# Turning the FFN's input with VectorE and small SBUF transfers instead of TensorE, and another order of work at the entry of the pool mixer

## The chip, the cores and the metric

The kernel runs on one core of a Trainium2 chip, in one launch. The metric is the device time of that core in microseconds. The core has five engines that run their own instruction queues in order: TensorE (PE, with its weight loads as PEld), VectorE (DVE), ScalarE (ACT), GpSimd (POOL) and SyncE (SP, which here issues nearly all DMA transfers). They wait for each other through semaphores.

## The reference

Two blocks follow each other on x of 1024 rows and 1024 columns, all in fp32. The first block is latent attention beside an mLSTM, then an FFN, then a gated per-layer embedding. The second block is a pooling mixer with a layer norm. What bears on the change:

```python
mix = jnp.concatenate([mla_out, mlstm_out], axis=-1) @ w_out[i]
h = h + rms_norm(mix, attn_post_norm[i])

f = rms_norm(h, ffn_pre_norm[i])
f = (jax.nn.silu(f @ w_gate[i]) * (f @ w_up[i])) @ w_down[i]
h = h + rms_norm(f, ffn_post_norm[i])
h = h + jax.nn.sigmoid(h @ w_ple_gate[i]) * (p[i] @ w_ple_proj[i])
# second block
h = x @ w_in                      # pool_mixer: 1024 x 4096
u, z = h[..., :D_POOL], h[..., D_POOL:]
outs.append((c - lag) / cnt - u[:, :, g])   # windowed means of u
```

## The kernel before

Matrix products are made with each fp32 operand split in a rounded part (hi, fp32r) and a rest (lo), as three products hi*hi, hi*lo, lo*hi (`three`). The big products of FFN and pool mixer use a seven-product scheme for 2x2 blocks (`quad`): a quad has seven block products o = 0 to 6 of 12 matmuls each. Products 4, 5 and 6 are added onto the banks in which products 0, 2 and 3 lie, so before each of them ACT must have copied that bank out (`copy_product`, counted by `prod_copied`), and DVE adds the copies up (`quad_sums`, counted by `quad_summed`).

**Output projection and FFN input.** The loop over the eight row tiles t of 128 rows works so. PE makes `mixed(t, 0)` and `mixed(t, 1)`, 24 matmuls each, into two PSUM banks that alternate between even and odd t. ACT takes the squares of the result with the 1024 x 128 tile `h1_blk` as a throwaway output (L2397), DVE scales it into `h1_blk` (L3191) and adds `x_blk` (L3195, `h1_ready`), splits the mixer rows of tile t+2 (`split_mix`), ACT takes squares again (L2403), and DVE writes `f_blk` = the FFN's input rows (L3201, `rows_ready`). PE then transposes `f_blk` by eight 128x128 products with the identity (`f_transposed`, L1731) into PSUM. ACT copies the result twice (`take_f`: L2385 to `f_full`, L2387 to the rounded part), and DVE subtracts to get the rest (`split_f`, L3182). PE transposes tile t-1 after `mixed(t, 1)`, and tile 7 inside the second gate block.

`x_blk` and `h1_blk` are single buffers. SP's program for tile t waits for `h1_ready`, spills `h1_blk` to DRAM (L889, `h1_spilled`), and loads `x_blk` for tile t+1 (L891, `xblk_in`). ACT's L2397 of tile t+1 waits for the spill of tile t (`act.wait_ge(h1_spilled, 16 * t)`), and DVE's L3195 waits for `x_blk`. PE's `mixed(t)` waits for L3191 of tile t-2 (`mix_taken`) and for the split of tile t (which stands behind L3195 of tile t-2).

**Pool entry.** The first two quads of the pool mixer (`N_QUADS`, `N_QUADS + 1`) start while the last gate product of the first block is still being used. The sums of x blocks that they need (`x_sums`, L3446 to L3452), their rounded parts (`x_sum_hi`, L2553) and rests (`x_sum_lo`, L3489) are made just in time. PE's order there is o = 0, 4, sum product 2, o = 5, sum product 1, and then the second quad with sum products 3 and 6 in between. ACT's order is written out by hand: rounded parts of x sums, copies of products (L2573), rounded parts of weights (`pool_block_hi`, `next_hi`, L2548), `silu` (L2639). POOL makes the rest of each weight block (L1327) after ACT has made its rounded part. DVE runs the x sums, the weight sums, `quad_sums` (L3256, L3260, L3262, L3275) and `window_rows` (L3538 to L3544) in one fixed order.

Of the kernel before, what the change touches and what calls it, by code (L numbers as in the profile page):

```python
# [25 lines left out]
P = 128  # L26
S = 1024
D = 1024
# [61 lines left out]
def build(nc, a, out):  # L90
    ctx = ExitStack()
    with ctx:
# [32 lines left out]
        def col(n):  # L125
# [117 lines left out]
            for j, name in enumerate(("e_buf", "d_t", "inter", "s_t", "q_in", "k_w")))  # L243
# [15 lines left out]
                 (r_10, r_01), f_part[0][1]]  # L259
        f_raw = [f_00, f_11, f_01, at("fs_raw3", [P, 4, HALF], Z)]  # L260
# [253 lines left out]
        def pool_landed(q):  # L514

            return 32 * ((12, 10)[q % 2] + q // 2 + 1)

# [163 lines left out]
        def sp_program(sp):  # L681
# [297 lines left out]
            def x3_store(i, n):  # L979

                sp.wait_ge(xr_ready, 4 * i + 2 * n + 2)
# [50 lines left out]
            for n in range(2):  # L1032
                sp.wait_ge(xr_stored[n], 64 * 4)
# [344 lines left out]
        def pe_program(pe):  # L1378
# [346 lines left out]
            def f_transposed(t):  # L1725
                pe.wait_ge(rows_ready, 8 + t + 1)
                if t >= 2:
                    pe.wait_ge(rows_split, 16 + 2 * t - 2)
                for k in range(KD):
                    b = 4 + 2 * (t % 2) + k // 4  # L1730
                    last = tr(ps[:, b, (k % 4) * P:(k % 4 + 1) * P], f_blk[:, k * P:(k + 1) * P], ident[:])  # L1731
                    if k % 4 == 3:
                        last.then_inc(rows_full, 1)
# [173 lines left out]
            def sum_product(o, at):  # L1907
# [6 lines left out]
                (w_h, w_l), (x_h, x_l) = ring[o], x_sum[i]  # L1914
                dst = ps[:, bank_of[o], :]
                for k in range(4):
                    cs = slice(k * P, (k + 1) * P)
                    mm(dst, w_h[:, cs], x_h[:, k, :], start=(o < 4 and k == 0), stop=False, skip_group_check=(o >= 4))
                    mm(dst, w_l[:, cs], x_h[:, k, :], start=False, stop=False, skip_group_check=(o >= 4))
                pe.wait_ge(xs_split, i + 1)  # L1920
                for k in range(4):
                    last = mm(dst, w_h[:, k * P:(k + 1) * P], x_l[:, k, :], start=False, stop=(k == 3),
                              skip_group_check=(o >= 4))
                last.then_inc(prod_full, 1)

# [9 lines left out]
            quad(N_QUADS, 0, x_factors, (0, 4), x_sums)  # L1935
            sum_product(2, 2)
# [82 lines left out]
        def act_program(act):  # L2019
# [371 lines left out]
            for t in range(TB):  # L2391
# [200 lines left out]
            def first_block_rows(i):  # L2592
                q = N_QUADS + 2 * i
                if i == 0:
                    act.wait_ge(xr_stored[1], 64 * 4)
                else:
                    act.wait_ge(m_stored[0], 16 * i)
# [11 lines left out]
            for i in range(8):  # L2609
# [17 lines left out]
                act.wait_ge(quad_summed, IN_SUMS + 4 * q + 2)  # L2627
                copy_product(q + 1, 4, 0)
                next_hi(q + 1, 0, 1)
                copy_product(q + 1, 4, 1)  # L2630
                next_hi(q + 1, 2)
                copy_product(q + 1, 4, 2)
                next_hi(q + 1, 3)
# [81 lines left out]
        def dve_program(dve):  # L2715
# [461 lines left out]
            def split_f(t):  # L3177
                for j in range(2):
# [3 lines left out]
                    v.tensor_tensor(f_l[:, :, ts], ps[:, 4 + 2 * (t % 2) + j, :].rearrange("p (k n) -> p k n", k=4),  # L3182
                                    f_h[:, :, ts].bitcast(F32), ALU.subtract).then_inc(rows_split, 1)
# [3 lines left out]
            for t in range(TB):  # L3187
# [15 lines left out]
                if t >= 1:  # L3203
                    split_f(t - 1)
# [250 lines left out]
            def x3_turned(j):  # L3455
# [3 lines left out]
                if i:  # L3459
                    dve.wait_ge(xr_stored[n], 64 * i)  # L3460
# [59 lines left out]
            dve.wait_ge(xr_stored[0], 64 * 4)  # L3520
# [8 lines left out]
            dve.wait_ge(xr_ready, 16)  # L3529
            dve.wait_ge(xr_stored[1], 64 * 4)  # L3530
# [293 lines left out]
```

## Time and profile before

| | |
|---|---|
| median of 3 runs | 1797.97 us (1797.95 to 1798.09) |
| the profiled execution's own time | 1797.84 us |
| its span, first to last instruction | 1796.0 us |
| granted TensorE clock, mean | 0.999 |
| busy: PE, DVE, POOL, ACT | 1777.2, 1410.6, 1102.2, 690.0 us |
| DMA | 206.53 MB, mean 115 GB/s |

The span is 1.8 us shorter than the execution's own time. PE is busy for 99% of the span, so the views that matter are those that tell in which stretches PE works on something that could go elsewhere, where it stands still, and what the other engines would do if it did not. Times of rows are in us from the start of the span; a row of the timeline gives the start, the duration, engine, line, operation, output<-input, shape and count, and in brackets the idle time of that engine before it and what ended it.

### The profile page before, as it was taken

The page shows a single profiled execution, that of the slowest core. Times are in us where ns is not written, and L with a number is a line of the kernel's source. Part 1 is how long each engine was busy: PE and PEld are TensorE (multiplying, and loading weights), DVE is VectorE, ACT ScalarE, POOL GpSimd, SP SyncE. Part 2 cuts the span into 40 slices and gives each one's busy share as a digit, 9 for nine tenths or more (in the row PEclk, how much of TensorE's full clock was granted, in tenths as well). Part 3 has the DMA queues.
Part 4 walks back from the last instruction along what each step waited for, and adds up shares of the span by engine and source line. Part 5 has one row for each costly group of instructions (what it writes and reads, how often), then busy time and mean ns, then how long its engine had stood idle before and what let it go on. Part 6 is the DMA issues. An engine that isn't in the chain of part 4 may idle for free.

```text
span 1796.0 us, 22436 instructions
## 1 busy us (share of the span) xinstructions
PE 1777.2 (99%) x8398; PEld 1485.6 (83%) x8398; DVE 1410.6 (79%) x1665; ACT 690.0 (38%) x1211; POOL 1102.2 (61%) x772
## 2 busy tenths in 40 slices
PE   9999999999999999999999999999999999999998
PEld 8888888888888888888888888887788888888886
DVE  7889877766696658666599989679888875798896
ACT  6555577843431111111233334414433343333314
POOL 4066632360399979888778778633655465567554
PEclk9999999999999999999999999999999999999999
DMA  7342410032303323233375631133232231943232
GB/s 210 95 154 57 126 34 17 22 125 94 128 27 103 129 71 118 96 116 117 106 281 179 231 129 48 48 98 90 94 123 100 106 141 71 366 173 107 73 102 94
DMA packets 142718, 206.53 MB, mean 115 GB/s; under 512 B 48897, under 2 KB 104833, under 8 KB 138897
## 3 DMA queue, kind: packets, MB, share of 16 engines
q1 hardware_dynamic: 142434, 205.03, 34.0%
q8 instruction: 67, 1.10, 0.2%
q14 instruction: 41, 0.34, 0.1%
q10 hardware_dynamic: 176, 0.07, 0.0%
HBM read 151.51 MB, written 53.04 MB: 114 GB/s over the span
## 4 chain that ended last, share of the span: by engine, by line
PE 77%; DVE 1%; ACT 1%; issue 0%; POOL 0%; DVEq 0%; ACTq 0%
PE ps L1392 68%; PE ps L1744 2%; PE ps L1746 2%; PE ps L1745 2%; PE ps L1978 1%; PE ps L1977 1%; PE ps L1979 1%; PE ps L1865 0%; ACT xs_hi L2553 0%; PE ps L1645 0%; PE ps L1731 0%; PE ps L1620 0%; PE ps L1635 0%; DVE xs_lo L3489 0%; POOL ring_lo L1327 0%
## 5 line engine op out<-in xcount | busy, mean ns | idle before, releaser
L1392 PE MATMUL ps<-f_hi,ring_hi 128*128 128x512 f32 x368 | 143.5, 390 | 0.0
L1392 PE MATMUL ps<-f_lo,ring_hi 128*128 128x512 f32 x368 | 143.3, 389 | 0.0
L1392 PE MATMUL ps<-f_hi,ring_lo 128*128 128x512 f32 x368 | 143.3, 389 | 0.0
L1238 POOL TENSOR_TENSOR ring_lo<-w_sum,ring_hi 128x512 fp32r<-128x512 f32 x84 | 128.4, 1529 | 7.0
L1392 PE MATMUL ps<-d_w_hi,d_hid_hi 128*128 128x512 f32 x312 | 121.6, 390 | 0.0
L2427 ACT ACTIVATE f_copy<-ps 128x512 f32<-128x512 f32 x63 | 37.3, 596 | 219.4 <-PE ps L1392 211.6
L1392 PE MATMUL ps<-d_w_hi,d_hid_lo 128*128 128x512 f32 x312 | 121.5, 389 | 0.0
L1392 PE MATMUL ps<-d_w_lo,d_hid_hi 128*128 128x512 f32 x312 | 121.5, 389 | 0.0
L1392 PE MATMUL ps<-f_low,ring_hi 128*128 128x512 f32 x336 | 117.2, 389 | 0.0
L1327 POOL TENSOR_TENSOR ring_lo<-w_sum,ring_hi 128x512 fp32r<-128x512 f32 x56 | 87.6, 1574 | 40.7 <-ACT ring_hi L2548 40.6
L1237 POOL TENSOR_SCALAR ring_hi<-w_sum 128x512 fp32r<-128x512 f32 x84 | 79.1, 942 | 31.3 <-PE ps L1392 30.2
L1392 PE MATMUL ps<-xs_lo,ring_hi 128*128 128x512 f32 x240 | 93.4, 389 | 0.0
L1392 PE MATMUL ps<-xs_hi,ring_hi 128*128 128x512 f32 x240 | 93.4, 389 | 0.0
L1392 PE MATMUL ps<-xs_hi,ring_lo 128*128 128x512 f32 x240 | 93.4, 389 | 0.0
L1237 POOL TENSOR_SCALAR ring_hi<-stage 128x512 fp32r<-128x512 f32 x37 | 34.2, 924 | 90.3 <-PE ps L1746 84.4
L1327 POOL TENSOR_TENSOR ring_lo<-stage,ring_hi 128x512 fp32r<-128x512 f32 x24 | 35.4, 1479 | 78.2 <-ACT ring_hi L2548 78.1
L1392 PEld LDWEIGHTS ps<-f_hi,ring_hi 128*128 128x128 f32 x368 | 69.1, 188 | 14.3
L1392 PEld LDWEIGHTS ps<-f_lo,ring_hi 128*128 128x128 f32 x368 | 69.1, 188 | 14.3
L1392 PEld LDWEIGHTS ps<-f_hi,ring_lo 128*128 128x128 f32 x368 | 69.1, 188 | 14.3
L1392 PE MATMUL ps<-x_hi,ring_hi 128*128 128x512 f32 x192 | 75.3, 392 | 4.7 <-ACT x_copy L2573 4.3
L1118 POOL TENSOR_TENSOR w_lo<-stage,w_hi 128x1024 fp32r<-128x1024 f32 x30 | 75.2, 2506 | 2.5
L2460 ACT ACTIVATE d_hid_hi<-d_raw 128x1024 fp32r<-128x1024 f32 x37 | 39.1, 1060 | 96.0 <-PE ps L1392 96.0
(574 smaller groups left out, 5859.8 us busy)
## 6 DMA issues: line engine op xcount, KB each, us to landing
d_raw<-hid_rows SPq DMA_DIRECT2D x37, 512.0 KB, 4.4
stage<-in_w_up SPq DMA_DIRECT2D x22, 512.0 KB, 4.6
wd_raw<-in_w_down SPq DMA_DIRECT2D x22, 512.0 KB, 5.0
raw_w<-in_w_gate SPq DMA_DIRECT2D x20, 512.0 KB, 4.9
stage<-in_pool_w_in SPq DMA_DIRECT2D x16, 512.0 KB, 4.9
raw_w<-in_pool_w_in SPq DMA_DIRECT2D x16, 512.0 KB, 4.7
m_rows<-u_row SPq DMA_DIRECT2D x16, 512.0 KB, 2.6
z_rows<-z_buf SPq DMA_DIRECT2D x8, 1024.0 KB, 4.1
```

Of the source, the lines that this page charges most:

```text
L1118: g.tensor_tensor(lo, stage[:, h, :], hi.bitcast(F32), ALU.subtract).then_inc(parted[h], 1)
L1237: pool_hi.do(pool, g.tensor_scalar(view(hi), src, 1.0, 0.0, ALU.mult, ALU.add))
L1238: g.tensor_tensor(view(lo), src, view(hi).bitcast(F32), ALU.subtract).then_inc(w_split, 1)
L1327: g.tensor_tensor(as_blocks(lo, src), src, as_blocks(hi, src).bitcast(F32), ALU.subtract).then_inc(w_split, 1)
L1392: last = mm(out_ap, l, r, start=(start and j == 0), stop=(stop and j == n - 1), skip_group_check=onto)
L1744: mm(o, l_hi, w_hi[s][:, c:c + HALF], start=(k == 0), stop=False)
L1745: mm(o, l_hi, w_lo[s][:, c:c + HALF], start=False, stop=False)
L1746: last = mm(o, l_lo, w_hi[s][:, c:c + HALF], start=False, stop=(k == 7))
L1977: mm(ps[:, m, :], w_hi[1][:, c:c + P], x_h, start=(k == 0), stop=False)
L1978: mm(ps[:, m, :], w_hi[1][:, c:c + P], x_l, start=False, stop=False)
L2427: f(copies[:, j, :], ps[:, bank0 + bank_of[o], :], ACT.Copy).then_inc(prod_copied, 1)
L2460: f(d_hid[s % 4][0][:], d_raw[s % 6][:], ACT.Copy).then_inc(d_hi, 1)
```

## The change

For rows tiles 0 to 5 (`TURNED = 6`) PE no longer transposes `f_blk`. DVE transposes it in 32x32 blocks into one of two new buffers (`f_turned`, 128 x 1024), and SP moves the blocks to their places in `f_full` with 16 transfers of 32 KB from SBUF to SBUF, each with runs of 128 bytes. ACT then makes the rounded part from `f_full` instead of from PSUM (one copy for each half instead of two), and DVE the rest. `take_f` and `split_f` work two tiles behind instead of one. Tiles 6 and 7 are transposed by PE as before. At the pool entry PE makes the rounded part of sum product 2 ahead of o = 4 and its rest behind it, and ACT's copies stand in another order: before the second to fourth rounded parts of x sum 1, and in the second quad after the first instead of the second sum of the quad before.

```diff
@@ sp_program, in the loop over t, behind the load of x_blk
+                if t < TURNED:
+                    sp.wait_ge(xr_ready, t + 1)
+                    for c in range(4):
+                        for b in range(4):
+                            rows = f_full[32 * c:32 * c + 32, :, t * P + 32 * b:t * P + 32 * b + 32]
+                            turned = f_turned[t % 2][32 * b:32 * b + 32, :].rearrange("c (k a r) -> c k a r", k=KD, r=32)
+                            sp.dma_start(rows, turned[:, :, c, :], **SMALL).then_inc(xr_stored[t % 2], 16)
@@ pe_program
             for t in range(2, TB):
                 pe.wait_ge(mix_taken, t - 1)
                 mixed(t, 0)
-                if t == 2:
-                    f_transposed(0)
                 mixed(t, 1)
-                f_transposed(t - 1)
+                if t > TURNED:
+                    f_transposed(t - 1)
...
-            quad(N_QUADS, 0, x_factors, (0, 4), x_sums)
-            sum_product(2, 2)
+            quad(N_QUADS, 0, x_factors, (0,), x_sums)
+            sum_high(2, 2)
+            quad(N_QUADS, 0, x_factors, (4,), x_sums, at=1)
+            sum_low(2)
@@ act_program
             def take_f(t):
                 for j in range(2):
+                    if t < TURNED:
+                        act.wait_ge(xr_stored[t % 2], moved(t))
+                        f(f_part[j][t // 4][0][:, :, (t % 4) * P:(t % 4 + 1) * P],
+                          f_full[:, 4 * j:4 * j + 4, t * P:(t + 1) * P], ACT.Copy).then_inc(rows_hi, 2)
+                        continue
...
-                if t >= 1:
+                if 1 <= t <= TURNED:
+                    act.wait_ge(xr_ready, t)
+                elif t:
                     act.wait_ge(rows_full, 16 + 2 * t)
...
-                if t >= 1:
-                    take_f(t - 1)
+                if t >= 2:
+                    take_f(t - 2)
+            take_f(TB - 2)
             take_f(TB - 1)
...
-            x_sum_hi(0, (0, 1, 2))
+            x_sum_hi(0)
             act.wait_ge(w_split, IN_BLOCKS + blocks_split(N_QUADS) + 7)
             copy_product(N_QUADS, 0, 0)
-            x_sum_hi(0, (3,))
             x3_part(15)
-            x_sum_hi(1)
+            x_sum_hi(1, (0,))
             copy_product(N_QUADS, 0, 1)
+            x_sum_hi(1, (1, 2, 3))
...
-                act.wait_ge(quad_summed, IN_SUMS + 4 * q + 2)
+                act.wait_ge(quad_summed, IN_SUMS + 4 * q + (2 if i else 1))
                 copy_product(q + 1, 4, 0)
+                if i == 0:
+                    next_hi(q + 1, 0)
+                    act.wait_ge(quad_summed, IN_SUMS + 4 * q + 2)
+                    copy_product(q + 1, 4, 1)
+                    copy_product(q + 1, 4, 2)
+                    next_hi(q + 1, 1, 2, 3)
@@ dve_program, in the loop over t, behind L3201
-                if t >= 1:
-                    split_f(t - 1)
+                if t < TURNED:
+                    dve.wait_ge(rows_ready, 8 + t + 1)
+                    if t >= 2:
+                        dve.wait_ge(xr_stored[t % 2], moved(t - 2))
+                    v.transpose(f_turned[t % 2][:], f_blk[:]).then_inc(xr_ready, 1)
+                if t >= 2:
+                    split_f(t - 2)
+            split_f(TB - 2)
             split_f(TB - 1)
```

## Rows read from the trace of the kernel before

**Rows 1.** The page's first part: busy us, share of the span, instructions.
```profile
PE 1777.2 (99%) x8398; PEld 1485.6 (83%) x8398; DVE 1410.6 (79%) x1665; ACT 690.0 (38%) x1211; POOL 1102.2 (61%) x772
```
**Rows 2.** Timeline around one transposition by PE (tile 1).
```profile
421.98 0.40 PE L1746 MATMUL ps<-w_hi,mix_lo 128*128 128x512 f32 x1
...
422.21 1.04 PE L1731 MATMUL ps<-ident,f_blk 128*128 128x128 f32 x8
...
423.00 0.47 PE L1744 MATMUL ps<-w_hi,mix_hi 128*128 128x512 f32 x1
```
**Rows 3.** Timeline of SP for one tile, and landing of a spill.
```profile
438.36 0.33 SPq L889 DMA_DIRECT2D h_rows<-h_blk  x1
438.73 0.43 SPq L891 DMA_DIRECT2D x_blk<-in_x_lanes  x1
...
h_rows<-h_blk SPq DMA_DIRECT2D x8, 512.0 KB, 2.9
```
**Rows 4.** SP's timeline where it issued 16 transfers from SBUF to SBUF.
```profile
45.94 5.04 SPq L743 DMA_DIRECT2D rot<-cos_q  x8
51.02 3.33 SPq L743 DMA_DIRECT2D rot<-neg_sin_q  x4
54.40 2.49 SPq L743 DMA_DIRECT2D rot<-sin_q  x4
56.93 1.13 SPq L687 DMA_DIRECT2D stage<-in_w_in  x2
```
**Rows 5.** Issues of other small transfers by tile: ns min/median/max.
```profile
L784 SPq DMA_DIRECT2D wqr_h<-in_w_uq x6: 434/469/470, 235.4 to 237.9; - x6
L986 SPq DMA_DIRECT2D x_rows<-x_turned x32: 303/498/1034, 1167.0 to 1252.9; - x32
```
**Rows 6.** Tile 0 of `f_blk` (timeline), and DVE's block transposes (by tile).
```profile
411.34 1.29 DVE L3201 SCALAR_TENSOR_TENSOR f_blk<-h_blk,cols,ffn_gain 128x1024 f32<-128x1024 f32 x1
...
L3462 DVE STREAM_TRANSPOSE x_turned<-pp x16: 698/703/706, 1160.8 to 1250.8; 128x512 f32<-128x512 f32 x16
```
**Rows 7.** Timeline of tiles 6 and 7, from the product to the transposition.
```profile
469.57 1.02 ACT L2397 ACTIVATE h_blk<-ps 128x1024 f32<-128x1024 f32 x1 [4.29 <-PE ps L1746]
...
481.37 1.03 ACT L2397 ACTIVATE h_blk<-ps 128x1024 f32<-128x1024 f32 x1 [4.31 <-PE ps L1746]
...
487.14 1.29 DVE L3201 SCALAR_TENSOR_TENSOR f_blk<-h_blk,cols,ffn_gain 128x1024 f32<-128x1024 f32 x1
...
488.35 1.28 DVE L3182 TENSOR_TENSOR f_lo<-ps,f_hi 128x512 fp32r<-128x512 f32 x2
488.48 0.86 PEld L1731 LDWEIGHTS ps<-ident,f_blk 128*128 128x128 f32 x8 [0.56 <-DVE f_blk L3201]
```
**Rows 8.** PE's timeline at the pool entry, the rows with idle time before them.
```profile
1237.23 0.47 PE L1392 MATMUL ps<-x_hi,ring_hi 128*128 128x512 f32 x1 [0.84 <-ACT x_copy L2573]
...
1244.33 0.47 PE L1392 MATMUL ps<-x_hi,ring_hi 128*128 128x512 f32 x1 [1.38 <-ACT x_copy L2573]
...
1267.56 0.47 PE L1392 MATMUL ps<-x_hi,ring_hi 128*128 128x512 f32 x1 [1.20 <-ACT x_copy L2573]
1271.46 0.47 PE L1392 MATMUL ps<-x_hi,ring_hi 128*128 128x512 f32 x1 [0.93 <-ACT x_copy L2573]
```
**Rows 9.** Timeline of DVE, ACT, POOL and PE up to the third quad.
```profile
1252.89 2.29 DVE L3489 TENSOR_TENSOR xs_lo<-xs_raw,xs_hi 128x2048 fp32r<-128x2048 f32 x1 [1.44 <-ACT xs_hi L2553]
...
1284.42 0.63 ACT L2639 ACTIVATE z_buf<-z_buf 128x512 f32<-128x512 f32 x1 [10.28 <-DVE z_buf L3262]
...
1286.62 1.45 POOL L1327 TENSOR_TENSOR ring_lo<-stage,ring_hi 128x512 fp32r<-128x512 f32 x1 [10.60 <-ACT ring_hi L2548]
...
1288.13 0.50 PE L1392 MATMUL ps<-x_hi,ring_hi 128*128 128x512 f32 x1
```
**Rows 10.** DVE's timeline: four x sums, without and with a POOL operation beside them.
```profile
1248.35 2.48 DVE L3450 TENSOR_TENSOR xs_raw<-pp 128x512 f32<-128x512 f32 x4
...
1255.10 3.59 DVE L3452 TENSOR_TENSOR xs_raw<-pp,xs_raw 128x512 f32<-128x512 f32 x4
```

More of the change, by code:

```diff
@@ L259, in build @@
                  (r_10, r_01), f_part[0][1]]
+        f_turned = [at(f"f_turned{i}", [P, D], Z + 4 * KB * i) for i in range(2)]
         f_raw = [f_00, f_11, f_01, at("fs_raw3", [P, 4, HALF], Z)]
@@ L516, in pool_landed, with moved @@
             return 32 * ((12, 10)[q % 2] + q // 2 + 1)
+        TURNED = 6
+        MOVED = TURNED // 2 * 16 * 16
+        def moved(t):
+            return 16 * 16 * (t // 2 + 1)
         X3_SPLIT = [j for j in range(16) if not (j < 8 and j % 4 >= 2)]
@@ L979, in x3_store @@
             def x3_store(i, n):
-                sp.wait_ge(xr_ready, 4 * i + 2 * n + 2)
+                sp.wait_ge(xr_ready, TURNED + 4 * i + 2 * n + 2)
                 for b in range(4):
@@ L1032, in sp_program @@
             for n in range(2):
-                sp.wait_ge(xr_stored[n], 64 * 4)
+                sp.wait_ge(xr_stored[n], MOVED + 64 * 4)
             for b in range(4):
@@ L1732, in f_transposed @@
                     if k % 4 == 3:
-                        last.then_inc(rows_full, 1)
+                        last.then_inc(rows_full, 2 * TURNED + 1 if t == TURNED and k == 3 else 1)
             def mixed(t, e):
@@ L1905, in pe_program, with sum_high @@
             sum_of = {2: 0, 1: 1, 3: 2, 6: 3}
-            def sum_product(o, at):
+            def sum_high(o, at):
                 i = sum_of[o]
@@ L1913, in sum_product @@
                 pe.wait_ge(xs_hi_ready, 4 * i + 4)
-                (w_h, w_l), (x_h, x_l) = ring[o], x_sum[i]
+                (w_h, w_l), x_h = ring[o], x_sum[i][0]
                 dst = ps[:, bank_of[o], :]
@@ L1919, in sum_product, with sum_low @@
                     mm(dst, w_l[:, cs], x_h[:, k, :], start=False, stop=False, skip_group_check=(o >= 4))
+            def sum_low(o):
+                i = sum_of[o]
                 pe.wait_ge(xs_split, i + 1)
                 for k in range(4):
-                    last = mm(dst, w_h[:, k * P:(k + 1) * P], x_l[:, k, :], start=False, stop=(k == 3),
-                              skip_group_check=(o >= 4))
+                    last = mm(ps[:, bank_of[o], :], ring[o][0][:, k * P:(k + 1) * P], x_sum[i][1][:, k, :], start=False,
+                              stop=(k == 3), skip_group_check=(o >= 4))
                 last.then_inc(prod_full, 1)
+            def sum_product(o, at):
+                sum_high(o, at)
+                sum_low(o)
             def x_sums(o):
@@ L2594, in first_block_rows @@
                 if i == 0:
-                    act.wait_ge(xr_stored[1], 64 * 4)
+                    act.wait_ge(xr_stored[1], MOVED + 64 * 4)
                 else:
@@ L2626, in act_program @@
                     next_hi(q, 4, 5, 6)
-                act.wait_ge(quad_summed, IN_SUMS + 4 * q + 2)
+                act.wait_ge(quad_summed, IN_SUMS + 4 * q + (2 if i else 1))
                 copy_product(q + 1, 4, 0)
[L2629 to L2633, printed above, removed]
+                if i == 0:
[4 more added lines that the diff above has]
+                    next_hi(q + 1, 1, 2, 3)
+                else:
+                    next_hi(q + 1, 0, 1)
+                    copy_product(q + 1, 4, 1)
+                    next_hi(q + 1, 2)
+                    copy_product(q + 1, 4, 2)
+                    next_hi(q + 1, 3)
                 if i == 7:
@@ L3181, in split_f @@
                     f_h, f_l = f_part[j][t // 4]
-                    v.tensor_tensor(f_l[:, :, ts], ps[:, 4 + 2 * (t % 2) + j, :].rearrange("p (k n) -> p k n", k=4),
-                                    f_h[:, :, ts].bitcast(F32), ALU.subtract).then_inc(rows_split, 1)
+                    src = ps[:, 4 + 2 * (t % 2) + j, :].rearrange("p (k n) -> p k n", k=4)
+                    if t < TURNED:
+                        src = f_full[:, 4 * j:4 * j + 4, t * P:(t + 1) * P]
+                    v.tensor_tensor(f_l[:, :, ts], src, f_h[:, :, ts].bitcast(F32), ALU.subtract).then_inc(rows_split, 1)
             split_mix(0, 1)
@@ L3202, in dve_program @@
                                        ALU.mult, ALU.mult).then_inc(rows_ready, 1)
[L3203 to L3204 removed]
+                if t < TURNED:
+                    dve.wait_ge(rows_ready, 8 + t + 1)
[5 more added lines that the diff above has]
+            split_f(TB - 2)
             split_f(TB - 1)
@@ L3459, in x3_turned @@
                 if i:
-                    dve.wait_ge(xr_stored[n], 64 * i)
+                    dve.wait_ge(xr_stored[n], MOVED + 64 * i)
                 turned = x_turned[n][:].rearrange("p (t m c) -> p m t c", m=2, c=32)[:, j % 2]
@@ L3519, in dve_program @@
                 x_sums(3, k)
-            dve.wait_ge(xr_stored[0], 64 * 4)
+            dve.wait_ge(xr_stored[0], MOVED + 64 * 4)
             second_sums((2,))
@@ L3527, in pool_sums @@
                 block_sums(N_QUADS + q, w_sum[q % 2], 3 - q % 2)
-            dve.wait_ge(xr_ready, 16)
-            dve.wait_ge(xr_stored[1], 64 * 4)
+            dve.wait_ge(xr_ready, TURNED + 16)
+            dve.wait_ge(xr_stored[1], MOVED + 64 * 4)
             for c in range(2):
```

## The prediction, made before the changed kernel was run

> **What bounds the kernel now.** I read the page's busy shares first, then PE's waits, then the timeline of two stretches. PE is busy for 99% of the span [rows 1]; the reader is to see that only two things shorten this kernel, matmuls that leave PE and stalls of PE. The longest stalls by cause are four waits for ACT's copies of products at the pool entry, 4.35 us in all [rows 8]. In the output projection PE never waits, and it spends part of its time on transposing. So both parts of the change aim at PE. The question is what the other queues do with their new work.
>
> **What goes from PE.** Between the last matmul of one half of the mixer and the first after the transposition lie 1.02 us; one matmul step is 0.23, so eight transposes hold 0.79, and the matmul behind them takes 0.47 in place of 0.39 [rows 2]. That is 0.87 us for one tile, and six tiles leave PE: 5.2 us.
>
> **What comes to SP.** For each of six tiles SP issues, behind the spill and the load of `x_blk`, 16 transfers, and the next tile's spill stands behind them in its queue. Spill and load themselves take 0.37 + 0.47 = 0.84 us of SP [rows 3]. A transfer from SBUF to SBUF of this size has rows in this trace: 16 of 32 KB over 32 partitions each, issued back to back, from 45.94 to the next issue at 56.93 [rows 4]. So 16 cost 10.99 us of SP: 0.63 each for the eight and the last four, and one group of four that took 0.84 longer. Other small transfers were cheaper to issue: 256 runs of 128 bytes from DRAM took a median of 0.47 (0.51 with the gap), 512 runs of 256 bytes to DRAM 0.50 [rows 5], thus 8.2 to 8.6 us for 16. I take 10.99, because it is the only row with SBUF at both ends, and the new transfers have the same bytes and partitions; their 256 runs instead of 32 could make it more. The bounds are 8.2 and, at 1.03 each as the slowest of [rows 5], 16.5 us.
>
> **What SP's time does to the end of the stage.** I follow SP's queue. Tile 0 of `f_blk` is written at 412.6 and its block transpose takes twice 0.70, so the first transfers start at 414.0 [rows 6]. A turn of SP is then 10.99 + 0.84 = 11.8 us. PE's turn is 11.80 (from L2397 of tile 6 to that of tile 7 [rows 7]), less 0.87 without transposes = 10.9 us. SP is the slower one and has no gap: h1 and the block transpose of each tile are ready before SP comes to them (tightest is tile 2: the spill of tile 1 starts at 425.0 and lands at 427.9; from L2397 to `f_blk` it is 7.1 [rows 7], under 1 for the split of mixer rows, 1.4 for the block transpose, so 437.3, and SP gets there at 437.7). Six sets of transfers and five pairs of spill and load end at 414.0 + 66.0 + 4.2 = 484.2. There the spill of tile 6 starts, lands 2.9 later [rows 3] at 487.1, and only then may ACT overwrite `h1_blk` for tile 7, which it did at 481.37 before [rows 7]. The last tile's chain is therefore 5.7 us later than before, although PE came to its end 5.2 us earlier. Everything that was taken from PE is spent in waits within `mixed` and behind the first gate block.
>
> **One more wait at the end.** PE's transposition of tile 7 waits until the rests of tile 5 are made. Before, DVE had made them a tile earlier. Now `split_f(5)` stands in tile 7's turn behind `f_blk`, 1.28 us [rows 7]. In PE's queue behind it stands the rest of the gate block, and for that all of the FFN. The stall of 0.56 there becomes 1.28 longer. The sum for the stage is +5.7 + 1.3 = +7.0 us. ACT's work falls (two copies for a tile instead of four) and DVE gets 1.4 more for a tile; both have 4.3 us of idle time in a turn, as ACT's 4.31 shows [rows 7], so they cost nothing. If that cover were gone each would cost 1.4 a tile. The landing of a tile's transfers isn't awaited for two turns, 22 us, and a spill of as many bytes lands in 2.9 [rows 3].
>
> **If the transfers are cheaper.** The same sum gives the point of decision: the stage costs nothing when 6B + 414.0 + 4.2 + 2.9 = 481.37 - 1.28, that is at B = 9.8 us for 16. Up to about 8.5 us nothing waits and the stage gives -5.2 + 1.3 = -3.9. At 16.5 it would be +7.0 + 6 x 5.5 = +40.
>
> **Pool entry.** The four waits are 0.84, 1.38, 1.20 and 0.93 [rows 8]. The first goes, since 8 matmuls now stand before the product that waits. Of the second about 0.9 stays: the copy can start only when the rest of sum product 2 is through. The third and fourth go, since their copies no longer stand behind DVE's second sum. PE would be 3.5 us ahead. But it can't keep that. Product 4 of the third quad started at 1288.13 right on POOL's rest of its weights, which waited 10.60 for ACT's rounded part, which stood behind the `silu` that waited 10.28 for DVE's sum [rows 9]. Nothing of this order is changed, and DVE works without a gap from 1252.89 to that sum. So what counts is how much earlier DVE starts at 1252.89, where it waited 1.44. The rounded parts that it waits for now come with DVE's own sums, which end some 0.7 later than before because `x_sum_lo(1)` has to wait for the parts that were moved behind the copy. That leaves -0.7. Against it, POOL's second block of that quad moves from DVE's idle time onto the four x sums, and such a meeting costs 3.59 - 2.48 = 1.1 [rows 10]. I take -0.3; the bounds are -2.0, all that DVE idles in this stretch with the 1.44, and +2.2, two such meetings more.
>
> The page "SBUF — State Buffer" of the Trainium skill, section "Who interferes with whom", says that a DVE instruction with two SBUF inputs and a GpSimd instruction that reads SBUF exclude each other for a whole instruction. The row agrees: 1.1 us more, close to one POOL operation. If it didn't hold, the entry would give -0.7 and not -0.3.
>
> The page "DMA: Bandwidth & Descriptors" of the Trainium skill, section "Issuing engines are not separate DMA queues", calls the sequencer's time to start a DMA "usually small relative to the DMA itself". By that SP's 11 us would not be counted and the change would give -4.2, which is the first rival below; [rows 4] speak against it.
>
> **Sum.** +7.0 - 0.3 = +6.7 us on the profiled execution's 1797.84 (span 1796.0 and 1.8 around it), 1804.5; on the median, 0.13 higher, 1804.7. I predict 1804.7 us.
>
> **Rivals.** (1) The transfers issue at the pace of [rows 5], 8.2 to 8.6 us for 16. SP's turn of 9.4 fits in PE's 10.9, and PE keeps its 5.2: -3.9 - 0.3 = -4.2, 1793.8. For it: 38 small strided transfers at a median of 0.47 and 0.50, with more runs each than [rows 4]. Against it: none of the three groups of [rows 4] went below 0.62 for a transfer, with only 32 runs in each. It decides below 8.5 us. (2) In between: only the usual 0.63 counts and the 0.84 extra of one group doesn't repeat: B = 10.1, and the stage costs 6 x 10.1 less 59.0 = +1.7. With fewer gaps, B = 9.3, it is about -1. Total 1797 to 1799.5. (3) The 256 runs make an issue dearer than any of [rows 4], 11.6 to 13 us for 16: 1808 to 1817. (4) DVE's order doesn't hold PE at the third quad and all 3.5 us of the entry stay: 3.2 less in each case, 1790.6 with rival 1. Against it [rows 9].
>
> **How the numbers follow.** Forecast 0.45, rival 1 0.26, rival 2 0.18, rival 3 0.09, rival 4 0.02. A measurement here tells from no change what is over 0.2%, 3.6 us. Faster: rivals 1 and 4, 0.28. Same: most of rival 2, 0.15. Slower: the rest, 0.57. Range 1793 to 1811, which leaves out rival 4, the low edge of rival 1 and the greater part of rival 3. The forecast's own range is 1801 to 1809.
>
> **What would show it.** In the timeline of SP, 16 issues for a tile that take about 11 us with no gap to the next spill, from 414 to 484; in the same stretch L2397 of each tile from 2 on waiting for the spill and not for PE; PE waiting in front of `mixed` and 12 us or so in all; PE's transposition of tile 7 at about 495.5 behind two L3182. At the entry, the four x_copy waits down to one of about 0.9, and a new one of some 3 us before product 4 of the third quad. Wrong it is if 16 issues take under 9.8 us, or if L2397 still follows PE directly.

## The result and the profile after

| | before | after |
|---|---|---|
| median, taken together | 1797.96 us (1797.8 to 1798.09, 4 runs) | 1811.17 us (1810.04 to 1812.63, 4 runs) |
| the profiled execution | 1797.84 us | 1812.63 us |
| its span | 1796.0 us | 1810.8 us |
| granted TensorE clock, mean | 0.999 | 0.994 |

The ratio is 1.0074, with a 95% interval from 1.0062 to 1.0086: 13.2 us slower. The forecast was 1804.7 us and its range ended at 1811. The direction was right, the size was half of what it is. The profiled execution is the slowest of the four, 14.8 us over that of before, so the positions below add up to 14.8 and not to 13.2.

First the page's busy times, against [rows 1].

```profile
PE 1779.3 (98%) x8350; PEld 1484.9 (82%) x8350; DVE 1420.9 (78%) x1671; ACT 685.4 (38%) x1199; POOL 1098.4 (61%) x772
```

PE has 48 transposes fewer and is busy for 2.1 us more. Waits can't do that, since they aren't busy time; matmuls that take longer can. Keep that in mind for the clock below.

SP's timeline in the output projection (start, duration, engine, line, operation, count), against [rows 3]:

```profile
414.01 10.48 SPq L906 DMA_DIRECT2D f_full<-f_turned  x16
424.54 0.60 SPq L897 DMA_DIRECT2D h_rows<-h_blk  x1
425.18 0.43 SPq L899 DMA_DIRECT2D x_blk<-in_x_lanes  x1
425.65 10.64 SPq L906 DMA_DIRECT2D f_full<-f_turned  x16
...
473.61 1.76 SPq L899 DMA_DIRECT2D x_blk<-in_x_lanes  x1
475.42 10.40 SPq L906 DMA_DIRECT2D f_full<-f_turned  x16
485.86 0.60 SPq L897 DMA_DIRECT2D h_rows<-h_blk  x1
```

SP never rests between 414 and 486. Sixteen issues take 10.40 to 11.42 us, 64.7 in all for the six sets; [rows 4] had said 10.99. Next the waits of the whole stage, from 400 on (engine, what waits, for whom: us in total, times, the longest), from two answers, of ACT and of PE. Before, PE had none here.

```profile
ACT h_blk L2426 <- DMA h_rows<-h_blk: 37.7, 6, 9.5
```
```profile
PE ps L1746 <- DVE f_lo L3224: 9.0, 2, 4.8
PE ps L1759 <- DVE mix_lo L3058: 3.9, 4, 1.2
```

L2426 is L2397 of before. From tile 2 on all six wait for the spill. PE pays 3.9 us in `mixed` and 9.0 in front of its two transpositions (L1746). The last tile, against [rows 7], with ACT, DVE and PE from three timelines:

```profile
489.27 1.02 ACT L2426 ACTIVATE h_blk<-ps 128x1024 f32<-128x1024 f32 x1 [5.39 <-DMA h_rows<-h_blk]
```
```profile
495.05 1.39 DVE L3242 SCALAR_TENSOR_TENSOR f_blk<-h_blk,cols,ffn_gain 128x1024 f32<-128x1024 f32 x1
496.36 2.76 DVE L3224 TENSOR_TENSOR f_lo<-f_full,f_hi 128x512 fp32r<-128x512 f32 x2
```
```profile
485.72 1.94 PE L1746 MATMUL ps<-ident,f_blk 128*128 128x128 f32 x8 [4.80 <-DVE f_lo L3224]
499.27 1.94 PE L1746 MATMUL ps<-ident,f_blk 128*128 128x128 f32 x8 [4.25 <-DVE f_lo L3224]
```

Eight transposes took 1.04 us in [rows 2]; here they take 1.94. The windows say why (from:to, length, busy time and count of PE, PEld, DVE, ACT and POOL, then PE's granted clock, DMA share and GB/s):

```profile
476.00:482.00 6.00, 4.92 (x22) 3.75 (x20) 2.67 (x3) 1.85 (x4) 5.75 (x6) 1.00 0.58 135
482.00:490.00 8.00, 4.28 (x14) 3.75 (x15) 2.65 (x4) 2.58 (x6) 0.56 (x1) 0.58 0.60 160
490.00:496.00 6.00, 5.02 (x22) 3.82 (x20) 3.78 (x5) 3.13 (x9) 1.17 (x2) 0.99 0.78 266
496.00:504.00 8.00, 4.73 (x16) 4.13 (x17) 6.52 (x8) 3.87 (x8) 5.40 (x4) 0.57 0.41 131
504.00:510.00 6.00, 6.00 (x28) 4.97 (x27) 5.86 (x5) 4.29 (x4) 3.77 (x3) 1.00 0.00 0
1300.00:1306.00 6.00, 4.64 (x13) 3.65 (x14) 2.50 (x5) 5.19 (x10) 5.27 (x5) 0.72 0.47 176
```

Three times the granted clock falls to the lower of its levels, 1.2 GHz, while PE stands or has just stood: at the stalls of 4.80 and 4.25 us and at one of 3.19 us at the pool entry. In the kernel before, each of these windows is at 1.00.

The pool entry, against [rows 9], from the timelines of DVE, ACT, POOL and PE:

```profile
1257.32 2.29 DVE L3536 TENSOR_TENSOR xs_lo<-xs_raw,xs_hi 128x2048 fp32r<-128x2048 f32 x1 [1.39 <-ACT xs_hi L2585]
1261.83 3.58 DVE L3497 TENSOR_TENSOR xs_raw<-pp 128x512 f32<-128x512 f32 x4
1266.11 2.29 DVE L3536 TENSOR_TENSOR xs_lo<-xs_raw,xs_hi 128x2048 fp32r<-128x2048 f32 x1
```
```profile
1297.68 0.63 ACT L2678 ACTIVATE z_buf<-z_buf 128x512 f32<-128x512 f32 x1 [11.25 <-DVE z_buf L3309]
```
```profile
1299.88 1.43 POOL L1342 TENSOR_TENSOR ring_lo<-stage,ring_hi 128x512 fp32r<-128x512 f32 x1 [10.60 <-ACT ring_hi L2580]
```
```profile
1301.36 0.50 PE L1407 MATMUL ps<-x_hi,ring_hi 128*128 128x512 f32 x1 [3.19 <-POOL ring_lo L1342]
```

The row at 1266.11 answers to the one at 1252.89, and the four x sums ahead of it to those of [rows 10]. This is the chain that [rows 9] showed, and PE now waits at its end.

Where the 14.8 us are, by matching matmuls of the two traces: PE's transposition of tile 7 is 10.8 us later (L2426 of tile 7 by 7.9, from it to the transposition 10.0 instead of 7.1). Behind the slow matmuls the shift is 12.8, and it stays so for 740 us ("shift" is, here and below, how much later a matmul starts than the same one of the kernel before). At the entry it falls to 10.2, rises to 13.2 at product 4 of the third quad and to 14.5 behind the third slow stretch.

### The profile page after: what moved, and what is told of

The parts are those of the page before. It is cut to its first block, busy times and chain, and to the rows that moved or that the text cites. A ratio compares the mean times of both kernels' runs of the same rounds, so it can differ in the third digit from the quotient of the medians.

```text
span 1810.8 us, 22443 instructions
## 1 busy us (share of the span) xinstructions
PE 1779.3 (98%) x8350; PEld 1484.9 (82%) x8350; DVE 1420.9 (78%) x1671; ACT 685.4 (38%) x1199; POOL 1098.4 (61%) x772
## 4 chain that ended last, share of the span: by engine, by line
PE 70%; DVE 4%; SPq 4%; ACT 1%; issue 1%; DMA 0%; POOL 0%; DVEq 0%; ACTq 0%
PE ps L1407 65%; SPq L906 3%; PE ps L2001 1%; PE ps L2002 1%; PE ps L2003 1%; ACT xs_hi L2585 0%; PE ps L1879 0%; DVE win L3585 0%; PE ps L1660 0%; DVE ln_dev L3636 0%; PE ps L1635 0%; PE ps L1761 0%; PE ps L1759 0%; PE ps L1760 0%; DVE xs_lo L3536 0%
## 5 line engine op out<-in xcount | busy, mean ns | idle before, releaser
L1407 PEld LDWEIGHTS ps<-f_lo,ring_hi 128*128 128x128 f32 x368 | 69.8, 190 | 14.5
L1407 PEld LDWEIGHTS ps<-f_hi,ring_lo 128*128 128x128 f32 x368 | 69.6, 189 | 14.6
```

The source lines that it names most:

```text
L1407: last = mm(out_ap, l, r, start=(start and j == 0), stop=(stop and j == n - 1), skip_group_check=onto)
```

## The experiments

Each kernel was timed in five rounds against the kernel before on the same chip. A difference in us is that of the two medians; a kernel that it names as its base is one told of earlier. The edits are cut down to the lines that matter, and lines in words stand for code. "The transposition part alone" is the first kernel below, and all kernels from there on leave the entry part out unless they say that they have it. Kernels with the same code carry other line numbers: L1731, L1744, L1746, L1748 and L1750 on `ident,f_blk` are all PE's transposition.

### The parts alone

Edit: the diff without its entry part (first kernel), and only its entry part (second kernel).

> The transposition part alone; the pool entry keeps the order of before. Theory: nearly all of the +13.2 us is made in the output projection (matching matmuls are 12.8 us late behind it), so +12.8 us, and the trace has the same late spills and the same two stretches of halved TensorE clock. Rival A, the two parts help each other (the entry order earns something only together with the late stage): more than +14. Rival B, the entry order alone costs more than the 1.8 us that the comparison of the traces shows: under +10.

Measured: 1809.53 us against 1797.87, +11.7; ratio 1.0067 (1.0055 to 1.0080). The same late spills, and in the profiled execution the same two stretches of slow clock (PE waits for rests 9.2 us in two stalls, 5.9 the longest). That execution was the slowest of the five, 1812.35 us; the fastest took 1808.46.

> The entry order alone; tiles 0 to 5 are transposed by TensorE as before. Theory from the two traces: PE gains 2.5 us at the four copies, gives 3.0 back in a wait for POOL's rest of product 4 of the third quad, and the clock falls to 1.2 GHz behind that stall for another 1.3 us: +1.8 us. My prediction had -0.3. Rival: the meeting of DVE and POOL in the changed kernel is an accident of the late stage, and alone the order gives -1 or better.

Measured: 1799.47 us, +1.6; 1.0009 (1.0000 to 1.0018). PE is 2.3 us ahead at its copies and 0.7 late at product 4 of the third quad, behind a wait of 3.2 for POOL. The clock didn't fall here, though the stall was as long as the 3.19; the rest of the loss came later (the shift grew from 0.7 to 1.9 between 1350 and 1403) and wasn't followed. The interval begins at 1.0000, so this loss only just stands clear of none. The parts add up: 11.7 + 1.6 = 13.3 against 13.2.

### What in SP's work costs the time

The base of both kernels is the transposition part alone. In the first, not all blocks come to their right places; the bytes and the runs are those of before.

```diff
-for c in range(4): for b in range(4):  rows = f_full[32*c:32*c+32, ...]; turned = f_turned[t % 2][32*b:32*b+32, :]
+for c in range(2): for b in range(4):  rows = f_full[64*c:64*c+64, ...]; turned = f_turned[t % 2][64*c:64*c+64, :]
```

> The transposition part alone, each tile's blocks moved by 8 transfers of 64 KB over 64 partitions instead of 16 of 32 KB over 32; the same bytes in the same runs of 128 bytes, but not all blocks come to their right places, so the FFN computes on a permuted input. Theory, SP's time to issue is the cause: if the cost is one for each transfer, 8 cost 5.4 us, SP's turn is 6.6 of PE's 10.9, no L2426 waits for a spill, and what stays is -5.2 and 1.3 to 2.8 of the later rests of tile 5: -4 to -2.5 us. Rival A, the cost goes by bytes or runs: 8 still take about 10.8 us and the result stays at +12.8. Rival B, traffic between SBUF ends or DVE's six block transposes are the cause: SP is free but the result stays above +5.

Measured: 1793.66 us, -4.2; 0.9978 (0.9969 to 0.9987). SP's timeline for one tile:

```profile
452.26 5.37 SPq L906 DMA_DIRECT2D f_full<-f_turned  x8
458.34 0.33 SPq L897 DMA_DIRECT2D h_rows<-h_blk  x1
458.71 0.43 SPq L899 DMA_DIRECT2D x_blk<-in_x_lanes  x1
```

Eight transfers with twice the bytes and twice the runs cost 0.67 each, as the sixteen did. So between these two forms an issue costs by the transfer, not by bytes, partitions or runs, and the traffic itself, the same here, holds up nothing. The spill's issue is back at 0.33 where SP stood idle before it; where it followed the transfers at once it took 0.62 in this kernel too. What still keeps this kernel from 5.2 is a wait of 1.4 us for rests in front of PE's transposition of tile 7.

```diff
-for c in range(4): SP issues the 4 transfers of c, behind the load of x_blk
+for c in range(3): SP issues the 4 transfers of c
+ACT, behind the root that follows L2426 of tile t (1 <= t <= 6): wait xr_ready >= t; issue c = 3 of tile t-1
```

> The transposition part alone, 12 of a tile's 16 transfers issued by SP and 4 by ACT, in ACT's wait for h1 of the next tile. Theory: SP's turn is 12 x 0.66 + 1.1 = 9.1 us, less than PE's 10.9, and ACT spends 4 x 0.65 = 2.6 us where it waited 2.9; no spill is late, PE keeps the 5.2 us but for the rests of tile 5 (1.3 to 2.8): -4 to -2.5 us. Rival A, two queues share one issuing resource, so 16 cost 10.8 us in sum whoever issues them: about +8 to +13. Rival B, ACT's issues delay its second squares and so the chain of each tile by 2 us or more: -1 to +3.

Measured: 1794.47 us, -3.4; 0.9983 (0.9975 to 0.9992). This lies in the theory's range. ACT's issues, first usual, last one disturbed:

```profile
456.03 2.71 ACTq L531 DMA_DIRECT2D f_full<-f_turned  x4
467.10 3.91 ACTq L531 DMA_DIRECT2D f_full<-f_turned  x4
```

Two queues issue side by side, ACT at SP's price. The Trainium skill's page "DMA: Bandwidth & Descriptors", section "Issuing engines are not separate DMA queues", says that starting DMAs on more engines saves only the sequencer's time, "usually small relative to the DMA itself". Here that time is all there is to save, and it is worth 15 us: 0.66 for a transfer that lands in 2.0 isn't small once there are 96.

### Order instead of load

First, PE's wait for the rests of tiles 4 and 5 goes from the transposition part alone (also part of the next kernels, where they say so); their sources no longer lie in the banks that PE writes.

```diff
 def f_transposed(t):
     pe.wait_ge(rows_ready, 8 + t + 1)
-    if t >= 2:
-        pe.wait_ge(rows_split, 16 + 2 * t - 2)
```

> The transposition part alone, and PE transposes tiles 6 and 7 without waiting for the rests of tiles 4 and 5, whose sources no longer lie in the PSUM banks that it writes. Theory: behind f_blk(7) DVE spent 2.8 us on the rests of tile 5 before PE could go on, where my prediction had 1.28; this goes, and the rest of the delay, the late spills, stays: 12.1 less 2.8, and less up to 1.3 if the second stretch at 1.2 GHz gets shorter with the stall, so +8 to +9.5 us. Rival: the block behind needs all rests anyway (gate block 2 waits for those of tile 7), so nothing is won: +11 to +12.5.

Measured: 1806.40 us, +8.5; 1.0049 (1.0037 to 1.0061). 3.2 us less than with the wait, as expected: the rests behind `f_blk(7)` were 2.8 us of the loss.

```diff
 sp, tile t: spill(t), load of x_blk,
-            16 transfers of tile t
+            16 transfers of tile t-1   (1 <= t <= 6)
```

> As the transposition part alone without the wait for rests (+8.5 us), but SP issues the 16 transfers of tile t-1 behind the spill of tile t and the load of x_blk, and not those of tile t ahead of the next spill. The number of issues and their cost stay. Theory: it is not SP's load as such but what stands behind it in the queue. SP's sixth set now ends behind the last spill that anything waits for; spill 6 starts at 476.5 and lands at 480, 3.8 us behind PE's 476.2, so -5.2 + 3.8 = -1.4, to within 1 us. Rival A, SP's total load decides whatever the order: +8.5. Rival B: the transfers of tile 5, which now end at 488.5, make its rests or the load of the next weight block late: +1 to +4.

Measured: 1805.68 us, +7.8; 1.0043 (1.0030 to 1.0056). A miss: the total is near rival A's, though the loss now comes about otherwise. My theory was that only the order in SP's queue is at fault, and for the stage itself it came close: PE's shift at the transposition of tile 7 is -0.2 where the base had +8.0. The spill isn't waited for any more, but others are: the copies of `f_full` wait for the landing of the transfers instead (an answer of ACT's waits), L2414 (L2426 of the changed kernel) stands behind them in ACT's queue, and at tile 7 it starts at 481.2, not at 480. That wait comes first, then PE's row at the transposition of tile 7 and POOL's at the next weight block:

```profile
ACT f_hi L2398 <- DMA f_full<-f_turned: 25.1, 6, 4.8
```

```profile
488.31 1.97 PE L1744 MATMUL ps<-ident,f_blk 128*128 128x128 f32 x8 [4.29 <-DVE f_blk L3223]
```
```profile
496.06 0.62 POOL L1252 TENSOR_SCALAR ring_hi<-stage 128x512 fp32r<-128x512 f32 x1 [17.50 <-DMA stage<-in_w_up]
```

`f_blk(7)` then came late for PE (4.3), the clock fell, and PE, 0.2 us ahead before it, was 2.0 late behind it. The weight block, loaded at 489.8 behind the last transfers, reached POOL late: 7.8 us behind the start of PE's transposition of tile 7, where in the base it was 1.7 us ahead of it. POOL's weight parts ran beside DVE's sums, and PE waited 0.6 for a rest and 2.7 at 513 for a copy of ACT and had the slow clock again; these bring the shift from 2.0 to 7.6. So most of the loss is what rival B named, the late weight block, at a higher price than its 1 to 4. That POOL's lateness made the wait at 513 is read from the timeline and wasn't tried by itself. SP's load, 11.8 us a turn, was waited for in this order too, behind other transfers.

### SP's share smaller, and fewer tiles

```diff
-for c in range(3): SP;  c = 3: ACT
+for c in range(4): SP issues 4 blocks for c < 3 and 2 for c = 3; ACT the other 2
+and no wait for the rests of tiles 4 and 5
```

> As the kernel with two queues, but SP issues 14 and ACT 2 of a tile's 16 transfers, and PE doesn't wait for the rests of tiles 4 and 5. With 12 and 4, ACT needed 3.91 us for four issues (0.98 each), PE stood 1.40 and 0.61 us for these rests, and the result was -3.4 us. Theory: SP's turn is 14 x 0.67 + 1.1 = 10.5 us of PE's 10.9, both stalls go, and PE keeps all of the 5.2: -5.2 to -4.7. Rival A: SP has no slack left at 10.5 and its spills drift late again: -3 or worse. Rival B: f_blk(7) is late by itself, so the stall only moves to it: -3.9.

The base is the kernel with two queues. Measured: 1800.90 us, +3.0; 1.0015 (1.0006 to 1.0024). Rival A. The expectation compared SP's turn with PE's, but SP starts late, at 414, and has to be through by a fixed time: PE's 476.2 for L2426 of tile 7 needs the spill of tile 6 at 472.8, so (472.8 - 414.0 - 5.6 for five pairs of spill and load) / 6 = 8.9 us for a set. Fourteen took 9.2 to 10.0, the spill started at 478.5 and L2426 at 481.9. Of the 5.7 us by which that spill is late, 3.7 come from the sets; in 1.7 more SP issued nothing between a spill and the next transfers, mostly because the block transpose that it waited for wasn't through, and the sum over the queue has no term for that. PE then stood 4.0 us for `f_blk(7)`, and the slow matmuls behind that stall cost 1.6. (I had also misread ACT's price in this expectation: 3.91 was its one disturbed set.)

```diff
-for c in range(3): SP;  c = 3: ACT        with the wait for rests
+the same, without the wait for the rests of tiles 4 and 5
```

> Two queues with 12 and 4 transfers (-3.4 us) and no wait for the rests of tiles 4 and 5. There PE stood 1.40 and 0.61 us for these rests. Theory: both stalls go, and PE, 2 us earlier, meets f_blk(7), written at 483.1, at 482.8 and waits 0.3: -5.1 us, 1792.9. Rival: the last tile's chain (its L2426 waits for the spill until 476.0 by SP's and ACT's issues) varies from run to run and takes a part: -4 to -3.4.

Measured: 1794.69 us, -3.2; 0.9980 (0.9972 to 0.9989). The rival: nothing is won over -3.4. PE's waits show the 2.0 us for rests turned into others:

```profile
PE ps L1748 <- DVE f_blk L3230: 1.1, 1, 1.1
PE ps L1411 <- DVE f_low L3265: 0.6, 1, 0.6
```

With the last tile's spill landing at 477.6, the last tile's chain is what holds PE.

```diff
-TURNED = 6
+TURNED = 2      (SP alone, with the wait for rests)
```

> The transposition part alone, for tiles 0 and 1 only; SP issues all. Theory: already one set of 16 is longer than the slack of the next spill. Spill 1 starts at 424.6, lands at 428.0, f_blk(2) is written at 435.1 and PE, which reaches its transposition of tile 2 at 432.5, waits 2.7; spill 2 lands at 439.8, and the rests of tile 1 behind f_blk(3) hold PE at tile 3 until 448.2, another 1.4. From there SP is free and the shift stays: -1.7 + 2.7 + 1.4 = +2.4 us, from +1.5 to +3. Rival: two tiles don't fill SP's queue, later turns take the delay up, and PE keeps 1.7: -1.7.

Measured: 1803.42 us, +5.6; 1.0032 (1.0021 to 1.0044). The loss needs no sum over six tiles. It comes with the first sets, and my estimate again left out the clock and a wait for rests in front of tile 2. PE's row at tile 2:

```profile
436.89 1.94 PE L1746 MATMUL ps<-ident,f_blk 128*128 128x128 f32 x8 [4.38 <-DVE f_lo L3207]
```

It takes 1.94 at the lower clock, and PE is 4.4 us late behind the slow matmuls; at tile 7 it stands 1.4 for the rests of tile 5, which DVE makes two tiles behind.

```diff
-TURNED = 6
+TURNED = 4      (SP 12, ACT 4, with the wait for rests)
```

> The kernel with 12 transfers from SP and 4 from ACT, for tiles 0 to 3 instead of 0 to 5. The kernels with six tiles came to -3.4 and -3.2 where PE's share alone would be -5.2; what was missing was lost at the last two transpositions and behind them. Theory: with two tiles of free queues between the last transfers and the last tile nothing waits at the end, so four tiles give their full 4 x 0.87 = 3.5: -3.5 to -3.0. Rival: the loss comes with the first PE transposition behind the transfers, wherever it stands, as 1.4 us of waiting for the rests of the tile two before: -2.1 or worse.

Measured: 1796.76 us, -1.1; 0.9994 (0.9985 to 1.0003). The rival: 1.1 us lost at the transposition of tile 4 and 1.4 at that of tile 7, both for rests.

```diff
-if t >= 2: take_f(t - 2)                 (ACT; DVE's split_f in the same way)
+if 2 <= t <= TURNED + 1: take_f(t - 2)
+if t > TURNED: take_f(t - 1)
-if t >= 2: pe.wait_ge(rows_split, 16 + 2 * t - 2)
+if t >= TURNED + 2: pe.wait_ge(rows_split, 16 + 2 * t - 2)
```

> The kernel with four tiles and two queues (-1.1 us; PE stood 1.1 at its transposition of tile 4 and 1.4 at that of tile 7, both times for rests that DVE makes two tiles behind), with two edits: PE doesn't wait for rests whose source isn't in its PSUM banks, and from tile 5 on ACT's copies and DVE's rests follow one tile behind again, as before the change. Theory: these two stalls are all that four tiles still lost, so PE keeps 3.5 less some tenths: -3.5 to -3.1 us. Rival: the stalls only move, to f_blk(4) or to the sums behind the gate block, as in the kernel with 12 and 4 for six tiles, which won nothing by the first edit: -1.5 to -1.

Measured: 1794.37 us, -3.6; 0.9980 (0.9971 to 0.9989). The theory's number, 4 x 0.87 = 3.5: PE keeps all of what four tiles give and waits for nothing in the stage. Of the kernels that move every block to its place it is the fastest, level with the six tiles on two queues, and it beats both kernels.

### The clock

```diff
 def f_transposed(t):
+    pe.wait_ge(rows_split, 16 + 8)        (the idle products read a part of tile 0 to 3)
+    for _ in range(20 if t == 6 else 24):
+        mm(ps[:, 4 + 2 * (t % 2), :], f_h[:, 0, 0:P], f_h[:, 0, :], start=True, stop=True)
     pe.wait_ge(rows_ready, 8 + t + 1)
```

> The transposition part alone (+12.1 us) with 20 and 24 idle products of 128x512 ahead of the transpositions of tiles 6 and 7, where PE stood 5.9 and 3.3 us; what they write is overwritten. Theory: the stalls stay where DVE's and SP's chain puts their ends, PE's clock doesn't fall to 1.2 GHz behind them, and the about 2 us go that the second slow stretch cost (the first is hidden in the next wait): +9.6 to +10.5. Rival A: the cost of the slow stretches is hidden, or comes from something else than PE's standing still: +12. Rival B: the clock falls all the same: +12 and the same halved clock in the windows.

The base is the transposition part alone. Measured: 1808.31 us, +10.4; 1.0059 (1.0047 to 1.0072), 1.3 us under the base's median. Its windows:

```profile
482.00:490.00 8.00, 6.59 (x34) 5.31 (x33) 3.19 (x7) 3.72 (x8) 0.00 (x0) 1.00 0.66 192
...
496.00:504.00 8.00, 8.00 (x41) 6.72 (x40) 6.83 (x8) 2.96 (x6) 3.85 (x3) 1.00 0.43 133
```

PE did useless work where it stood before, and the clock stayed at its higher level, 2.4 GHz. In the base the shift grew from 12.0 to 14.6 us over the slow matmuls behind tile 7; here it stays at 10.6. That the clock falls because PE stands still is shown by the windows, and by all five executions of either kernel: the mean granted clock is 0.999 or 1.000 here and 0.995 to 0.998 in the base. What it costs is shown by the shifts, and for the profiled execution alone, which in the base was the slowest of five. The shift ahead of the slow matmuls differs too (10.6 and 12.0), and the intervals of the two ratios overlap, so the times alone don't tell the kernels apart.

### The entry

```diff
 ACT, i == 0, behind the rounded parts of the second quad:
+    next_hi(q + 1, 4)
+    act.wait_ge(quad_summed, IN_SUMS + 4 * q + 5)
+    copy_product(q + 2, 0, 0)
     act.wait_ge(quad_summed, IN_SUMS + 4 * q + 6)
     silu(z_buf 3), silu(z_buf 0)
-    copy_product(q + 2, 0, 0)
-    next_hi(q + 1, 4)
```

> The entry order alone, and in ACT's order the rounded part of product 4 of the third quad and the copy of that quad's product 0 stand ahead of the silu that waits for DVE's sum. Theory: the 3.0 us given back at this product came from this wait and nothing else, so PE keeps its lead of 2.3 us there; with the later drift of 1.1 that the entry order alone showed, -1.2 to -2.3 us against before. Rival A: the next thing of the same DVE chain (its sums in front of the fourth quad) takes the lead back: -0.5 to +1. Rival B: POOL or the landing of the weights is the real holder: +1.6 as without it.

The base is the kernel with the entry part alone. Measured: 1801.61 us, +3.7; 1.0019 (1.0011 to 1.0028). Rival A, and worse than it said. Product 4 does start 2.6 us early. But POOL's rest of its weights, put earlier, now runs beside one more of DVE's window operations (L3562 took 1.13 us, in the base 0.16), DVE's sums end 1.0 later, the weights of product 5 stand behind them, and PE waits for that one:

```profile
PE ps L1392 <- POOL ring_lo L1327: 4.6, 1, 4.6
```

That stall halves the clock from 1291 to 1298. DVE's chain carries the third quad's weights one after another; freeing one exposes the next.

> The whole change with the three repairs: 14 transfers from SP and 2 from ACT, no wait for the rests of tiles 4 and 5, and the rounded part and the copy of the third quad ahead of the silu. If the parts add up: the sum of the two kernels before this in the list, -6.4 to -7.5 us, 1790.4 to 1791.5. Rival: the entry's lead is taken back by DVE's chain: -4.7, and with the entry as costly as alone -3.5.

Edit: the kernel with 14 and 2, this entry, no wait for rests. Measured: 1803.22 us, +5.3; 1.0031 (1.0019 to 1.0043). Neither case: both of its parts had missed, and +3.0 and +3.7 come together to +5.3.

> The kernel with 12 and 4 transfers and without the wait for rests, with the entry order of the changed kernel besides. If the parts add up, the order costs here what it cost alone, 1.6: -5.1 + 1.6 = -3.5. Rival: the entry order pays where the stage before it is not late: under -5.1.

Edit: the kernel with 12 and 4 without the wait for rests, and the entry order of the changed kernel. Measured: 1795.54 us, -2.4; 0.9987 (0.9978 to 0.9996). The order costs 0.8 beside the kernel without it, less than alone, though the intervals overlap. It doesn't pay.

## Why the prediction was half right

The direction and the path of the loss were forecast: SP's issues delay the spills, and PE waits at the end of the stage. The size failed in four terms of the sum, the time of spill and load behind the transfers (with the landing), the time of the last rests, the sum of the entry's two terms, and the slow matmuls behind a stall, for which no term stood.

**What bounds the kernel, and what goes from PE.** Right. The four caught-up tiles gave 3.6 us where 4 x 0.87 is 3.5 [rows 2].

**What comes to SP.** B = 10.99 was right: 10.8 on the mean. The nearest row had the same bytes and partitions and SBUF at both ends. Bytes, partitions and runs turned out not to matter between 16 and 8 transfers; whether SBUF at both ends is why these issues cost more than the 0.47 of [rows 5], no run tried. The 0.84 us for spill and load [rows 3] was mis-sized. Behind a transfer the spill's issue takes 0.60 and not 0.33, the pair 1.11 with the gaps, and once the load took 1.76. So the spill of tile 6 started at 485.9, not at 484.2: the pairs took 2.7 us more than the 4.2, the transfers 1.0 less than the 66.0.

**SP's time to the end of the stage.** The mechanism was right: L2426 of all tiles from 2 on waits for the spill. The spill took 3.4 to be seen instead of 2.9 and L2426 of tile 7 came 7.9 us late, not 5.7. Mis-sized by 2.2 us, of which 1.7 lie in SP's queue and 0.5 in the landing.

**The step of one more wait at the end.** The order was right (the rests of tile 5 behind `f_blk(7)`), the term was not: 1.28 was the duration of two subtractions with PSUM as one source [rows 7], and the change itself moves that source to SBUF. With both inputs in SBUF, the same two took 1.25 us in the two-queue kernel where POOL was idle, and 2.79 and here 2.76 where POOL made weight parts beside them. The two with PSUM as a source, started at 499.05 beside POOL's weight parts, took 1.27. The Trainium skill's page "SBUF — State Buffer", section "Who interferes with whom", says that a DVE instruction with two SBUF inputs contends with a GpSimd instruction that reads SBUF, and one with at most one SBUF input does not; these numbers agree with it. I had used this rule at the entry, [rows 10], and not here. Off by 1.6 us, 1.5 of them beside POOL. Without this wait the loss was 3.2 us smaller.

**What no step had.** The granted clock. The prediction took every stall at its length. PE's busy time grew by 2.1 us although 5.2 us of its work had gone; of the slow stretches the first is hidden in the next wait, the second costs 2.0 us and the one at the entry 1.3. These are sizes of the profiled execution; the other three were 1 to 3 us faster, with a mean clock of 0.995 or 0.996 against its 0.994, and have no trace.

**"If the transfers are cheaper".** The formula names the right deadline, the time by which the last spill is needed, and I forgot it for the kernel with 14 and 2. It isn't complete: with that kernel's mean of 9.5 for a set it puts L2426 of tile 7 at 478.0, and 481.9 was measured. The rest is 1.4 for the pairs, 0.5 for the landing, 1.7 in which SP stood idle, and gaps. Two of its figures were also worked out wrongly. For PE to keep its 5.2 us a set may take 9.2 us by the prediction's own terms, not 8.5, and 8.9 with the measured pairs and landing; twelve, at 7.9 to 9.1, just fit. And at the 9.3 of rival 2 the formula gives -3.2 us for the stage, not -1, so the low end of that rival was 1794.5.

**Pool entry.** The steps were seen as written: the x_copy waits fell from 4.35 to 1.2 us, DVE waited 1.39 at the same place, POOL met the four x sums (3.58), and PE gave the lead back at product 4 of the third quad. The two terms were right and I put them together wrongly. An earlier start of 0.7 and a meeting of 1.1 make +0.4, not -0.3: DVE's L3536 at 1266.11 is 0.5 late beside the stage's 12.8, and so is product 4. The clock took 1.3 more behind that stall.

Together: 6.7 forecast; + 2.2 (SP and landing) + 1.6 (rests, 1.5 of them beside POOL) + 2.0 (clock, stage) + 0.8 (entry) + 1.3 (clock, entry) = 14.6 of the profiled execution's 14.8. Rival 1 gave -4.2 us for a queue of SP that fits in PE's turn, and the kernel with eight transfers came to just that; but its own condition, an issue at the price of [rows 5], wasn't met.

## What to carry to other kernels

A queue that issues DMAs is an engine with a turn of its own: multiply the transfers by the time of one issue, add what else it issues at the price it has behind them and the time that it stands waiting for its next input, and set the sum against the time by which the last thing behind it is needed, not against the bound engine's turn. Spread over two queues, kept out of the last tiles, with the rests one tile behind again and without the entry part, this change gives 3.6 us instead of costing 13. Where a forecast ends in a stall of PE of several us, add the slow matmuls behind it, and where a copy moves from PSUM to SBUF, ask what POOL does beside its readers.

## What the runs showed of the hardware

- A transfer from SBUF to SBUF cost SP 0.65 to 0.71 us to issue, as the mean of a set, for 32 KB over 32 partitions with 256 runs, and 0.67 or 0.68 for 64 KB over 64 with 512; on ACT's queue 0.65 to 0.68 in four of six sets of the two-queue kernel, 0.74 and 0.98 in the others. A spill of 512 KB took 0.33 us to issue on an idle SP and 0.60 to 0.63 right behind these transfers, once 1.52.
- The granted clock fell at every PE stall of 4.0 to 5.9 us in these kernels, and at none of up to 1.8. Between 2.7 and 3.3 us it went both ways: it fell at five (2.7, 2.7, 3.19, 3.2, 3.3) and stayed at two (3.2 in the kernel with the entry order alone, 3.3 in the one without the wait for rests). While it was low, a matmul step took 0.43 us instead of 0.23 and eight transposes 1.94 instead of 1.04.
- Block transposes on DVE took 1.25 us for 128x1024, less than the 2 x 0.70 of two halves.
